# Input projection of a decoder layer: the norm's gain and its per-token factor move from x to the weights and to the PSUM eviction

## What is computed

```python
def rmsnorm(x, g):
    xf = x.astype(jnp.float32)
    y = xf * lax.rsqrt(jnp.mean(xf * xf, axis=-1, keepdims=True) + EPS)
    return (y * g.astype(jnp.float32)).astype(x.dtype)

def project(h, w_in_l):                      # h = rmsnorm(x, g_mix_pre), 1024 wide
    proj = jnp.einsum('btd,de->bte', h, w_in_l)      # w_in 1024 x 2560
    aq, ak, av, bq, bk, bv, cb, cc, cx = jnp.split(proj, IN_SPLITS, axis=-1)
```

## Time and profile before

| | us |
|---|---|
| median of three timed executions | 2756.61 |
| lowest, highest | 2752.45, 2758.62 |
| the profiled execution, its own time | 2758.52 |
| its span | 2756.7 |
| TensorE busy in the span | 2602.6 (94%) |
| start of the first matmul of block 1 | 96.7 |
| start of `attend` | 558.0 |

### The profile page before, as it was taken

How to read it: one execution, slowest core, us unless ns; L and a number is a source line. 1 busy time by engine, 2 the same in 40 slices (tenths; PEclk the granted TensorE clock), 3 DMA queues, 4 the chain that set the end, 5 groups by cost and what they waited for, 6 DMA issues and landing times.

```text
span 2756.7 us, 34953 instructions
## 1 busy us (share of the span) xinstructions
PE 2602.6 (94%) x13943; PEld 2248.6 (82%) x13943; DVE 737.5 (27%) x1604; ACT 977.4 (35%) x1670; POOL 1316.3 (48%) x839
## 2 busy tenths in 40 slices
PE   6999999969997969999999999999999989999995
PEld 4899999969996538788887888877888878898894
DVE  5421111056663233511112111142111252112112
ACT  4211221068775533422333233243233243232231
POOL 4200000046772456655555577476567365654453
PEclk8999999989998989999999999999999999999998
DMA  4311322189976964524444454354454344433331
GB/s 138 113 39 57 121 69 79 48 162 192 170 117 146 271 206 165 192 94 153 137 139 153 153 175 141 107 181 148 147 181 137 107 161 137 153 123 107 107 122 69
DMA packets 263447, 373.29 MB, mean 135 GB/s; under 512 B 78714, under 2 KB 197930, under 8 KB 258630
## 3 DMA queue, kind: packets, MB, share of 16 engines
q1 hardware_dynamic: 241136, 256.51, 33.4%
q10 hardware_dynamic: 15526, 93.82, 9.6%
q0 software_dynamic: 6624, 20.72, 2.7%
HBM read 322.96 MB, written 103.75 MB: 155 GB/s over the span
## 4 chain that ended last, share of the span: by engine, by line
PE 52%; POOL 4%; issue 3%; ACT 2%; DVE 1%; ACTq 0%; DMA 0%; POOLq 0%; DVEq 0%
PE ml_y L1673 30%; PE ml_up L1638 7%; PE ml_up L1640 7%; PE ml_up L1639 7%; POOL ml_w_lo L1551 1%; POOL em_y L1547 1%; ACT ml_square L1767 1%; POOL ml_a_lo L1560 1%; PE ml_y L1668 1%; POOL em_hx L1547 1%; DVE em_hx L1947 1%; PE ml_y L1667 1%; PE ml_up L1623 1%; PE ml_up L1611 0%; DVE em_y L1947 0%
## 5 line engine op out<-in xcount | busy, mean ns | idle before, releaser
L1551 POOL TENSOR_TENSOR ml_w_lo<-em_raw,ml_w_hi 128x1024 fp32r<-128x1024 f32 x288 | 700.7, 2434 | 478.1 <-ACT ml_w_hi L1701 477.8
L1701 ACT CAST ml_w_hi<-em_raw 128x1024 fp32r<-128x1024 f32 x288 | 301.7, 1048 | 573.1 <-PE ml_y L1673 358.8
L1673 PE MATMUL ml_y<-ml_w_hi,ml_a_hi 128*128 128x512 f32 x1216 | 475.6, 391 | 1.4 <-POOL ml_w_lo L1551 1.4
L1638 PE MATMUL ml_up<-ml_h_hi,ml_w_hi 128*128 128x512 f32 (+1 forms) x1280 | 454.3, 355 | 23.4 <-POOL ml_w_lo L1551 23.4
L1673 PE MATMUL ml_y<-ml_w_hi,ml_a_lo 128*128 128x512 f32 x1216 | 473.4, 389 | 0.0
L1673 PE MATMUL ml_y<-ml_w_lo,ml_a_hi 128*128 128x512 f32 x1216 | 473.3, 389 | 0.0
L1640 PE MATMUL ml_up<-ml_h_hi,ml_w_lo 128*128 128x512 f32 (+1 forms) x1280 | 452.3, 353 | 0.0
L1639 PE MATMUL ml_up<-ml_h_lo,ml_w_hi 128*128 128x512 f32 (+1 forms) x1280 | 452.1, 353 | 0.0
L1638 PEld LDWEIGHTS ml_up<-ml_h_hi,ml_w_hi 128*128 128x128 f32 x1280 | 241.6, 189 | 60.8 <-POOL ml_w_lo L1551 30.6
L386 PE MATMUL pj_acc<-pj_h_hi,pj_w_hi 128*128 128x424 f32 (+1 forms) x800 | 289.6, 362 | 1.0 <-DVE pj_h_lo L580 1.0
L387 PE MATMUL pj_acc<-pj_h_lo,pj_w_hi 128*128 128x424 f32 (+1 forms) x800 | 285.4, 357 | 0.0
(11 more groups left out here) (230 smaller groups left out, 3532.1 us busy)
## 6 DMA issues: line engine op xcount, KB each, us to landing
em_raw<-in_w_up SPq DMA_DIRECT2D x64, 1024.0 KB, 5.3
em_raw<-in_w_down SPq DMA_DIRECT2D x64, 1024.0 KB, 5.2
out_o_a_k_s<-in_cache_a_k ACTq DMA_DIRECT2D x8, 3060.0 KB, 13.2
out_o_a_v_s<-in_cache_a_v ACTq DMA_DIRECT2D x8, 3060.0 KB, 12.6
em_raw<-scratch_pt SPq DMA_DIRECT2D x36, 512.0 KB, 7.6
em_raw<-in_w_out SPq DMA_DIRECT2D x16, 1024.0 KB, 5.1
scratch_pt<-pj_proj SPq DMA_DIRECT2D x10, 1056.0 KB, 4.1
pj_w<-in_w_in SPq DMA_DIRECT2D x20, 512.0 KB, 4.0
```

The costliest lines, as they stand in the source:

```text
L1551: nc.gpsimd.tensor_tensor(split_of(w_lo, n), raw_of(n), f32(split_of(w_hi, n)), ALU.subtract).then_inc(w_lo_ready, 1)
L1638: pe.matmul(out, hi[:, k, :], h_hi[:, k, cols], start=(k == 0), stop=False)
L1673: last = pe.matmul(out, p[:, f, t0:t0 + m], w[:, b, :], start=(f == 0 and p is act_hi and w is hi), stop=(f == PF - 1 and p is act_lo))
L1701: nc.scalar.copy(split_of(w_hi, n), raw_of(n)).then_inc(w_hi_ready, 1)
```

## The change

Four things change in `project`:

1. **x is turned as it was loaded.** The gain product on GpSimd, the reciprocals and the products on VectorE go. Squares are summed on ScalarE for even tiles and on VectorE (`tensor_tensor_reduce`) for odd ones, and nothing in the front waits for them. x has eight slots, four in `work` and four in `proj`, with one semaphore per tile.
2. **The gain goes into the weights.** SP loads it as 8 rows of 128, TensorE turns it to a 128 x 8 tile, and GpSimd multiplies each of the 20 weight blocks by it in place (`scale_weights`, 128 x 1024) before `split_hi`. The 18 spreading DMAs stand behind the fourth of these.
3. **The norm factor is multiplied at eviction.** After the last tile one root, one reciprocal, five products of the identity with the factors (`diag`) on VectorE, five float32 matmuls with a tile of ones (`spread`) on TensorE and five copies on ScalarE give `rstd_of`, in which every partition holds the factors of all 2112 tokens. `evict` is on VectorE for all five groups, one `scalar_tensor_tensor` each: PSUM times `scale` times `rstd_of`.
4. **Order of small things.** The identity is loaded first; the constant `scale` has its own semaphore; the second weight block is loaded after the eighth tile of x; weight block 1 is split at tile 10, not 2; the four DMAs of the new sample rows (`store_new`) are issued while block 15 runs and only waited for at the end.

The diff, cut to what these four need:

```diff
+        def x_of(t):
+
+            y = t % X_SLOTS
+            at = work[:, y * D:(y + 1) * D] if y < 4 else proj[:, (y - 4) // 2, (y - 4) % 2 * D:((y - 4) % 2 + 1) * D]
+            return at[0:rows_of(t), :]
...
+        def load_x(engine, t):
+            if t >= X_SLOTS:
+                engine.wait_ge(turned_ready, 2 * (t - X_SLOTS + 1))
+                wait_squared(engine, t - X_SLOTS)
+            engine.dma_start(x_of(t), xs if t == TILES else xp[t]).then_inc(x_in[t], 16)
...
-            def load_x(t):
-                if t >= 2:
-                    sp.wait_ge(squared, t - 1)
-                    sp.wait_ge(xg_ready, t - 1)
-                n = rows_of(t)
-                sp.dma_start(x[0:n, t % 2, :], xs if t == TILES else xp[t]).then_inc(x_in[t % 2], 16)
...
+            def store_new():
+                for s in range(ROWS):
+                    sp.wait_ge(rows_out[s], rows_out_before(NROWS + (s - NROWS) % ROWS))
+                for out, c0, wd, n in ((d["o_a_k_s"], 0, AW, PAST), (d["o_a_v_s"], AW, AW, PAST),
+                                       (d["o_b_k_s"], 2 * AW, KVW, BWIN), (d["o_b_v_s"], 2 * AW + KVW, KVW, BWIN)):
+                    dst = out[0].rearrange("b t h e -> b t (h e)")[:, n - DEC_T:n, :]
+                    sp.dma_start(dst, d["kv"][SEQ:, c0:c0 + wd].rearrange("(b t) c -> b t c", t=DEC_T)).then_inc(new_out, 16)
...
-            load_x(0)
-            sp.dma_start(gain, d["g_mix_pre"].partition_broadcast(P)).then_inc(gain_in, 16)
-            load_x(1)
             sp.dma_start(ident[:], d["c_ident"]).then_inc(const_in, 16)
-            sp.dma_start(scale[:], d["c_scale"]).then_inc(const_in, 16)
+            load_x(sp, 0)
+            load_x(sp, 1)
             load_w(0)
-            load_w(1)
+            sp.dma_start(gain_rows, d["g_mix_pre"].rearrange("l (k p) -> (l k) p", p=P)).then_inc(gain_in, 16)
             for t in range(2, XT):
-                load_x(t)
+                load_x(sp, t)
+                if t == X_SLOTS - 1:
+                    load_w(1)
+                    sp.dma_start(scale[:], d["c_scale"]).then_inc(scale_in, 16)
...
+                if i == KV_FIRST + KV_BLOCKS + 2:
+                    store_new()
...
-            def scale_gain(t):
-                n = rows_of(t)
-                if t == 0:
-                    pool.wait_ge(gain_in, 16)
-                pool.wait_ge(x_in[t % 2], 16 * (t // 2 + 1))
-                if t >= 2:
-                    pool.wait_ge(turned_ready, 2 * (t - 1))
-                nc.gpsimd.tensor_tensor(xn[0:n, t % 2, :], x[0:n, t % 2, :], gain[0:n, :], ALU.mult).then_inc(xg_ready, 1)
-
-            for t in range(XT):
-                scale_gain(t)
+            nc.gpsimd.memset(ones[:], 1.0).then_inc(ones_ready, 1)
+            def scale_weights(i):
+                pool.wait_ge(w_in[i % 2], 16 * (i // 2 + 1))
+                if i == 0:
+                    pool.wait_ge(gain_ready, 1)
+                nc.gpsimd.tensor_tensor(w[:, i % 2, :, :], w[:, i % 2, :, :], gain[:].unsqueeze(2).to_broadcast([P, DBLK, P]),
+                                        ALU.mult).then_inc(w_scaled, 1)
+
+            for i in range(4):
+                scale_weights(i)
             for s in range(2):
                 pool.wait_ge(source_out[s], 16 * (NCHUNK // 2))
             for what, cols in (("near", NEAR_COLS), ("far", FAR_COLS)):
                 for h in range(source_heads(what)):
                     frm = bass.AP(source[what].tensor, h * cols, [[0, P], [1, cols]])
                     pool.dma_start(d[f"spread_{what}"][h], frm).then_inc(spread_out, 16)
+            for i in range(4, FBLK):
+                scale_weights(i)
...
-                pe.wait_ge(xn_ready, t + 1)
+                pe.wait_ge(x_in[t], 16)
...
+            def spread(c):
+                z = 2 * XT + c
+                if c < 3:
+                    pe.wait_ge(lo_ready, z - 2)
+                else:
+                    pe.wait_ge(rstd_spread, c - 2)
+                pe.wait_ge(diag_ready, c + 1)
+                pe.wait_ge(ones_ready, 1)
+                n = spread_chunk(c)[1]
+                m = min(n, P)
+                pe.matmul(turned[z % 3][:, 0:n], ones[0:m, :], diag[0:m, c * SPREAD * P:c * SPREAD * P + n],
+                          start=True, stop=True).then_inc(spread_ready, 1)
+
+            turn(0)
             pe.wait_ge(table_in, 16)
             pe.wait_ge(table_ones, 1)
             pe.wait_ge(state_in, 32)
+            pe.wait_ge(gain_in, 16)
+            pe.transpose(acc[3][:, 64:64 + DBLK], gain_rows, ident[0:DBLK, 0:DBLK])
...
+            for c in range(NSPREAD):
+                spread(c)
...
             def square(t):
-                n, s = rows_of(t), t % 2
-                act.wait_ge(x_in[s], 16 * (t // 2 + 1))
-                act.wait_ge(squared, t)
-                if t >= 2:
-                    act.wait_ge(rstd_ready, t - 1)
-                nc.scalar.activation(proj[0:n, 0, 0:D], x[0:n, s, :], ACT.Square, scale=D ** -0.5, accum_out=sumsq[0:n, s:s + 1]).then_inc(squared, 1)
-                act.wait_ge(squared, t + 1)
-                nc.scalar.activation(rms[0:n, s:s + 1], sumsq[0:n, s:s + 1], ACT.Sqrt, bias=eps[0:n, :]).then_inc(rms_ready, 1)
+                n = rows_of(t)
+                act.wait_ge(x_in[t], 16)
+                act.wait_ge(act_squared, squares_before(t))
+                act.wait_ge(mean_filled, 1)
+                nc.scalar.activation(rstd_of[0:n, 0:D], x_of(t), ACT.Square, scale=D ** -0.5,
+                                     accum_out=mean[0:n, t:t + 1]).then_inc(act_squared, 1)
...
-            def evict(i, g):
-                act.wait_ge(acc_ready, i * NG + g + 1)
-                if g == 0:
-                    wait_slot_free(act, i)
-                c0, n = COLS[g]
-                f = ORDER[i]
-                nc.scalar.activation(proj[:, i % 2, c0:c0 + n], acc[g][:, 0:n], ACT.Copy, scale=scale[:, f:f + 1]).then_inc(even_out, 1)
+            def copy_spread(c):
+                c0, n = spread_chunk(c)
+                act.wait_ge(spread_ready, c + 1)
+                nc.scalar.copy(rstd_of[:, c0:c0 + n], turned[(2 * XT + c) % 3][:, 0:n]).then_inc(rstd_spread, 1)
...
+            act.wait_ge(act_squared, ACT_SQUARES)
+            act.wait_ge(dve_squared, XT - ACT_SQUARES)
+            nc.scalar.activation(rms[:], mean[:], ACT.Sqrt, bias=eps[:]).then_inc(rms_ready, 1)
+            for c in range(NSPREAD):
+                copy_spread(c)
...
-            def normalise(t):
-                n, s = rows_of(t), t % 2
-                dve.wait_ge(rms_ready, t + 1)
-                if t >= 2:
-                    dve.wait_ge(xn_ready, t - 1)
-                nc.vector.reciprocal(rstd[0:n, s:s + 1], rms[0:n, s:s + 1]).then_inc(rstd_ready, 1)
-                dve.wait_ge(rstd_ready, t + 1)
-                dve.wait_ge(xg_ready, t + 1)
-                nc.vector.tensor_scalar(xn[0:n, s, :], xn[0:n, s, :], rstd[0:n, s:s + 1], None, ALU.mult).then_inc(xn_ready, 1)
+            def square(t):
+                n = rows_of(t)
+                dve.wait_ge(x_in[t], 16)
+                dve.wait_ge(mean_filled, 1)
+                dve.wait_ge(dve_squared, squares_before(t))
+                nc.vector.tensor_tensor_reduce(rstd_of[0:n, D:2 * D], x_of(t), x_of(t), 1.0 / D, 0.0,
+                                               ALU.mult, ALU.add, mean[0:n, t:t + 1]).then_inc(dve_squared, 1)
+
+            def invert():
+                dve.wait_ge(rms_ready, 1)
+                nc.vector.reciprocal(rstd[:], rms[:]).then_inc(rstd_ready, 1)
+                dve.wait_ge(rstd_ready, 1)
+                dve.wait_ge(turned_ready, 2 * XT)
+                for c in range(NSPREAD):
+                    n = spread_chunk(c)[1]
+                    m = min(n, P)
+                    to = diag[0:m, c * SPREAD * P:c * SPREAD * P + n].rearrange("p (t m) -> p t m", m=m)
+                    shape = [m, n // m, m]
+                    by = rstd[0:m, c * SPREAD:c * SPREAD + n // m].unsqueeze(2).to_broadcast(shape)
+                    nc.vector.tensor_tensor(to, ident[0:m, 0:m].unsqueeze(1).to_broadcast(shape), by, ALU.mult).then_inc(diag_ready, 1)
...
-                nc.vector.tensor_scalar(proj[:, i % 2, c0:c0 + n], acc[g][:, 0:n], scale[:, f:f + 1], None, ALU.mult).then_inc(odd_out, 1)
+                if i == 0:
+                    dve.wait_ge(rstd_spread, NSPREAD if g == NG - 1 else -(-(c0 + n) // (SPREAD * P)))
+                    dve.wait_ge(scale_in, 16)
+                if i == 0 and g == 0:
+                    dve.wait_ge(const_in, 16)
+                nc.vector.scalar_tensor_tensor(proj[:, i % 2, c0:c0 + n], acc[g][:, 0:n], scale[:, f:f + 1], rstd_of[:, c0:c0 + n],
+                                               ALU.mult, ALU.mult).then_inc(acc_out, 1)
...
-            normalise(0)
             for t in range(XT):
-                if t + 1 < XT:
-                    normalise(t + 1)
+                if not squared_by_act(t):
```

(7 more changed lines are left out.)

105 lines of the change are left out of this document (52 added, 53 removed).

## The result

| us | before | after |
|---|---|---|
| median of timed executions | 2757.61 (2752.45 to 2761.77, 4) | 2739.98 (2735.30 to 2745.51, 4) |
| profiled execution, its own time | 2758.52 | 2739.19 |
| its span | 2756.7 | 2737.2 |
| first matmul of block 1 | 96.7 | 82.2 |
| issue of the last store to start of attention | 10.37 | 5.31 |

The gain between the medians is 17.6 us; the forecast was 15.2.

A forecast was written before the change was run, and what follows sets the result against it. The front was held by the loop of turns and products over two slots, the blocks by matmuls. Front 10.5 plus end 4.7 gave 15.2 us: 2743.3 profiled, 2741.4 median, range 2732 to 2753.

The forecast's parts named there:

- What bounds the kernel: Projection: blocks bound by matmuls; front by the loop turn, gain product, norm product over two slots, with 19.6 us waits.
- The walk of TensorE's queue: Front, start to block 1: terms for tiles, products, gap and spreads summing to 82.2 us, before 96.7.
- the drain: Table load ahead of the root: about 1.38 us extra per change of set by the skill, left out of the sum.
- The allowance for the clock: Products of block 0: two of three begin at the lower clock, so block 1 starts at 86.2 us, not 82.2.
- Rival (b): Front: turns don't hold TensorE's clock, block 1 starts at 95.4, gain 6.0 us, time 2750.6; chance 0.22.
- TensorE's busy share between products: Sign in the front's spells of turns between products of block 0: the share was to be above 0.75.
- VectorE's square: Front, each second square of x on VectorE: taken as 1.3 us, between bounds of 1.06 and twice 1.22.
- Rival (d): Front: VectorE's square takes 2.4 us beside GpSimd, half of eight between products, 4.4 us, time 2745.8; chance 0.08.
- Costed at nothing: Blocks: evictions on VectorE, 20 weight gain products of 2.36 us on GpSimd, and 18 later spreading DMAs cost nothing.
- The end: End of the projection: the four DMAs issued early save 2.95 to 6.4 us; middle taken, 4.7.
- The blocks: Blocks after block 0: matmul-bound, 450 us without idle time, no change in length.
- The sum: Front 10.5 plus end 4.7 gives 15.2 us gain: 2743.3 for the profiled execution, 2741.4 for the median.

The follow-up runs named there:

- run 3: Kernel before without GpSimd's gain product on x, the 18 spreading DMAs held until the last tile is normalised: block 1 at 87.1 us, attention at 547.06.
- run 4: Changed kernel with two slots for x instead of eight, second weight block and `scale` loaded behind the third tile: block 1 at 91.1 us, attention at 546.61.
- runs 6: Changed kernel with the last product of block 0 ahead of the five spread matmuls: 2744.62 us, block 1 at 83.6.
- 7: Changed kernel with the gain's eight rows loaded first on ScalarE's queue instead of fifth on SP's: 2750.08 us, block 1 at 86.1.
- 11: Changed kernel with 13 unused bfloat16 matmuls ahead of the first turn and 8 behind it, to raise the clock: 2747.35 us, block 1 at 83.8.
- runs 9: Changed kernel with squares of tiles 5 to 14 beside the products and the last product ahead of the spreads: 2734.14 us, block 1 at 73.9.
- 10: Changed kernel with squares beside the products and the last product ahead of the spreads, timed in rounds: median 2734.35 us, ratio 0.9907 to the kernel before.
- Run 2: Kernel before with GpSimd's gain product on x left out, spreading DMAs not held: block 1 at 95.3 us.
- run 1: Kernel before with only the four DMAs of the new sample rows issued during block 15: attention 5.61 us behind the last store's issue, not 10.37.
- run 12: Kernel before with all five evictions of a block on VectorE instead of two: block 1 at 95.4 us, attention at 556.61.

## Why the prediction was right, and where its terms were off

**What bounds the kernel.** Right in the main. The loop through both products and two slots held the front, and the blocks kept their pace but for 1.2 us. Runs 3 and 4 take it apart: GpSimd's product 8 to 10 us, the slots 7 to 9. They don't add up to the 14.5: the first is what its absence gives with two slots, the second what their lack costs without it. The prediction took the mean of 1337 ns for what VectorE's product costs; it is 0.75 us alone, so a good part of that wait was GpSimd's work too (run 3). One reading was wrong: TensorE was not busy for 60 to 70% in every spell ahead of a product that began low. In two of them, in the kernel before, it was busy for 0.47 and 0.56 (length, busy):

```profile
59.00:67.10 8.10, 3.78 (x26) 0.81 0.41 138
73.50:83.60 10.10, 5.69 (x34) 0.70 0.47 118
```

**The walk of TensorE's queue.** It said 82.2 with the clock up in the three products behind the first, and the profiled execution started block 1 at 82.20. Term by term, forecast and measured: first table product ended 11.6 and 11.7; product 0 began 26.0 and 25.7; product 0 6.1 and 7.0; tiles 5 to 7 6.7 and 7.1; tiles 8 to 10 5.1 and 4.9; tiles 11 to 14 7.3 and 7.0; tiles 15 and 16 2.1 and 2.5; gap 3.9 and 3.6; spreads 6.7 and 5.6. The exact hit is luck: product 0 was 0.9 too short, the spreads 1.1 too long. The table load and the root in that gap:

```profile
L574 ACT ACT_TABLE_LOAD x1 | 1.3, 1283 | 0.0
L574 ACT ACTIVATE pj_rms<-pj_mean,pj_eps 128x17 f32<-128x17 f32 x1 | 0.3, 311 | 0.0
```

The root starts 0.02 us behind the load, without the drain that the prediction weighed against its row, so keeping to the row was right.

**The allowance for the clock.** On top of the walk stood 4 us for two products that lose the clock, hence 86.2. One execution had none (82.2), the other exactly two, at 1.5 us each and not 2, beside a first product 0.5 shorter (84.4). In runs 6, 7 and 11, whose three spells are much like these (5 to 8 us), two of the three lost it as well. So the count was right in four executions of five, the size a third too large, and the profiled execution was a fortunate one: the front gained 14.5 us in it and 12.3 in the second, not 10.5. The spread of the changed kernel's whole times is another matter: of the 8.9 us between the spans of its two profiled executions 2.7 lie ahead of attention and 6.2 behind. Rival (b), that turns don't hold the clock, is half true: 16.3 us of turns and table products with TensorE busy for 15.64 of them didn't raise it, and run 11's raised clock fell in them; but behind a product it lasted through the spell and the whole next product in 7 of the 15 cases of these five executions, and in all 6 of runs 9 and 10, whose spells are 4 to 6 us. The rule that the prediction named (the Trainium skill, TensorE: Matmul & The Clock Gate, section Part 4: PE-mode transpose) agrees with the former.

**A mark that missed.** TensorE's busy share between products was to be above 0.75. It was 0.74, 0.68 and 0.67 (5.16 of 7.0, 3.41 of 5.0, 4.76 of 7.1), against 0.68, 0.47 and 0.56 before, and with the same shares the clock held in one execution and fell in the other. So that share doesn't tell which way a spell goes.

**VectorE's square.** Forecast 1.3; alone it takes 1.2, beside GpSimd's gain product more than twice that:

```profile
51.24 2.86 POOL L377 TENSOR_TENSOR pj_w<-pj_w,pj_gain 128x1024 f32<-128x1024 f32 x1 [30.20 <-DMA pj_w<-in_w_in]
...
51.12 1.23 DVE L649 TENSOR_TENSOR pj_w_lo<-pj_w,pj_w_hi 128x1024 fp32r<-128x1024 f32 x1 [0.25 <-ACT pj_w_hi L541]
52.27 2.92 DVE L614 CUSTOM_DVE_ANT_0 pj_rstd_of<-pj_work 128x1024 f32<-128x1024 f32 x1
```

Rival (d) had the mechanism and the wrong count: it happened once in the profiled execution, since GpSimd has four gain products in the front. What the prediction lacked is the place of the squares: ahead of `lo_tile`, they stood between a full bank and its release, and run 9 shows what that cost.

**Costed at nothing.** The eviction with a second SBUF input took 0.66 us, at the lower end of 0.65 to 1.3. The weights' gain product took 1.90 us alone, not 2.36. No cost of the spreading DMAs shows here, but for a reason that the prediction didn't give: they went out at 58.2 to 67.7 us, into the loop's time, with a DMA share of 0.91 in the product at 61.3, and found all of x loaded. They stand behind the fourth gain product, whose weights SP loads behind x (the last load of x was issued at 45.59), and this held with two slots too (run 4). Run 2 shows their price where loads of x are still to come.

**The end.** Forecast 4.7 as the middle of 2.95 to 6.4; 5.1 in the changed kernel and 4.8 alone in run 1.

**The blocks.** Forecast unchanged; they are 1.2 us shorter, from the first matmul of block 1 to the issue of the last store 449.7 against 450.9. The difference lies where rows are turned back: seven such blocks take 24.8 us each instead of 24.9, and the plain ones 22.9 in both. The evictions are not the cause (450.9 in run 12), and half of it varies: the second execution of the changed kernel took 450.3, and so did run 3, which keeps the evictions of before. The cause is open.

**The sum.** For the profiled execution it was 2743.3, and 2739.19 were measured. The front gave 4.0 us more than forecast, the end 0.4 and the blocks 1.2; 1.3 were lost behind the start of attention, where nothing was forecast and where executions differ by 12 us. That the median came within 1.4 us is therefore in part luck; that it is faster, and by the front and the end, is not.

## To carry over

Read a loop's cost by what stands in it, then ask what the freed engine will do next: here GpSimd's early DMAs took back in run 2 nearly all that its missing products had given. Where work has no reader soon (squares for a norm that is applied late), put it beside the long matmuls, not ahead of the step that frees a buffer: moving ten squares and one product gave 7 to 10 us with no instruction less. And run an unchanged kernel a second time before explaining 2 us: it may be the clock.

## What the runs showed of the chip

- TensorE's clock: equal programs with equal gaps (1.8 us the longest) kept it in one execution and lost it in another, at 1.5 us for each product. Behind spells of 5 to 8 us of turns 7 products of 15 ran at the upper clock throughout, behind spells of 4 to 6 us all 6. Raised by 4.1 us of bfloat16 matmuls, it fell again within float32 work, 2.5 us behind a gap of 1.82 us.
- VectorE beside GpSimd, both reading SBUF: the one that began later did most of its work behind the other's end. A 128 x 1024 subtraction began at 20.14 beside a GpSimd product of 19.77 to 21.67 and ended 1.08 us behind it (2.61 in all; 1.22 alone); a square began at 52.27 beside one that ended at 54.10 and ended 1.09 behind it (2.92; 1.22 alone). That GpSimd product took 2.86 instead of 1.90, and 1.75 of it lay behind the end, at 52.35, of a subtraction that VectorE had begun first.
- GpSimd's 128 x 1024 product with the gain broadcast along the row took 1.90 us, against 2.36 in the mean with two full inputs.
- 18 DMAs from DRAM to DRAM brought the DMA share to 1.02 for 10 us. The four loads of x from 55 to 80 us took 7.9 us from issue to landing in the median, against 3.6 with the DMAs held (run 3).
